# Filling TensorE's waits in the first stage of a two-layer decoder trunk with zero products, and taking that stage in another order

## The reference, cut to what matters

```
mod_all = jnp.einsum('bd,lde->lbe', jax.nn.silu(c), w_mod) + b_mod[:, None]
shift1, scale1, gate1, shift2, scale2, gate2 = jnp.split(mod_all[i], N_MOD, axis=-1)
h = rms_norm(x, norm_g[i, 0]) * (1.0 + scale1[:, None]) + shift1[:, None]
# pooling mixer: causal means over 2, 4, 8, 16 tokens minus the token, by group of 256 channels
pooled = jnp.stack([mean_w(h_g) - h_g ...], axis=2)
y = jnp.einsum('bsgc,gce->bsge', pooled, w_grp).reshape(B, S, D) * scale
x = x + gate1[:, None] * rms_norm(y, norm_g[i, 1])
h = rms_norm(x, norm_g[i, 2]) * (1.0 + scale2[:, None]) + shift2[:, None]
y = swiglu(h, ffn_w_gu[j], ffn_w_down[j])
```

## Time and profile before

| | |
|---|---|
| median of 3 runs | 1278.63 us (1278.04 to 1280.4) |
| profiled execution | 1280.07 us |
| its span, first to last instruction | 1278.2 us |
| mean granted TensorE clock | 0.991 |
| PE busy | 1249.0 us (98%) |
| DVE, ACT, POOL busy | 387.3, 214.7, 109.8 us |
| moved by DMA | 477.47 MB, mean 374 GB/s |
| first product of the SwiGLU starts | 70.39 us |

### The profile page before, as it was taken

How to read it: one execution, slowest core, us unless ns; L and a number is a source line. 1 busy time by engine, 2 the same in 40 slices (tenths; PEclk the granted TensorE clock), 3 DMA queues, 4 the chain that set the end, 5 groups by cost and what they waited for, 6 DMA issues and landing times.

```text
span 1278.2 us, 31266 instructions
## 1 busy us (share of the span) xinstructions
PE 1249.0 (98%) x14625; PEld 779.1 (61%) x14625; DVE 387.3 (30%) x591; ACT 214.7 (17%) x320; POOL 109.8 (9%) x134
## 2 busy tenths in 40 slices
PE   6799999999999999999999999999999999999997
PEld 3589999989774354545455454554545545454555
DVE  1567778979872110101101011010101201011012
ACT  3253333474842000000000000000000000000001
POOL 4220000010030000020010010002001000200100
PEclk9899999999999999999999999999999999999999
DMA  9998998959379999999999999999999999999980
GB/s 371 414 358 295 334 333 305 364 197 395 123 245 420 425 423 425 424 402 424 424 407 424 424 409 411 424 409 404 423 421 396 422 424 412 404 424 415 399 355 36
DMA packets 114055, 477.47 MB, mean 374 GB/s; under 512 B 10944, under 2 KB 37280, under 8 KB 113792
## 3 DMA queue, kind: packets, MB, share of 16 engines
q1 hardware_dynamic: 106112, 457.29, 89.1%
q0 software_dynamic: 7664, 17.87, 4.6%
q10 hardware_dynamic: 144, 0.26, 0.1%
HBM read 465.79 MB, written 11.16 MB: 373 GB/s over the span
## 4 chain that ended last, share of the span: by engine, by line
PE 95%; DVE 2%; ACT 1%; POOL 1%; DMA 1%; issue 1%; SPq 0%; DVEq 0%; ACTq 0%
PE ps L2421 23%; PE ps L2407 23%; PE ps L2396 23%; PE ps L1927 7%; PE ps L1928 7%; PE ps L1929 7%; PE ps L1952 1%; PE ps L2014 1%; PE ps L1911 1%; DMA raw<-w_mod 1%; DVE wlo L1572 1%; PE ps L2205 1%; PE ps L1975 0%; PE ps L2035 0%; PE ps L2350 0%
## 5 line engine op out<-in xcount | busy, mean ns | idle before, releaser
L1799 DVE TENSOR_TENSOR act_in<-act_in,ps 128x1344 f32<-128x1344 f32 x16 | 24.9, 1555 | 527.1 <-PE ps L2407 527.1
L1927 PE MATMUL ps<-thi,whi 128*128 128x256 f32 x480 | 136.0, 283 | 0.8 <-DVE wlo L1421 0.8
L1928 PE MATMUL ps<-tlo,whi 128*128 128x256 f32 x480 | 135.8, 283 | 0.0
L1929 PE MATMUL ps<-thi,wlo 128*128 128x256 f32 x480 | 135.8, 283 | 0.0
L2396 PE MATMUL ps<-raw,turned_in 128*32 128x448 f32 x1296 | 123.7, 539 | 0.0
L2407 PE MATMUL ps<-ring_w,turned_in 128*32 128x448 f32 x1248 | 120.6, 539 | 0.0
L2421 PE MATMUL ps<-ring_w,turned_act 128*32 128x256 f32 x2016 | 117.2, 379 | 0.0
L2421 PE MATMUL ps<-raw,turned_act 128*32 128x256 f32 x2016 | 115.5, 379 | 0.0
L1220 ACT ACTIVATE act_in<-ps 128x1344 f32<-128x1344 f32 x16 | 20.7, 1292 | 548.6 <-PE ps L2396 548.6
L1290 DVE TENSOR_TENSOR wlo<-raw,whi 128x2048 fp32r<-128x2048 f32 x41 | 92.9, 2289 | 32.7 <-ACT whi L901 32.7
L2421 PEld LDWEIGHTS ps<-raw,turned_act 128*32 128x32 f32 x2016 | 82.4, 110 | 33.5 <-issue 3.5
(11 more groups left out here) (324 smaller groups left out, 1332.0 us busy)
## 6 DMA issues: line engine op xcount, KB each, us to landing
raw<-moe_w_gu SPq DMA_DIRECT2D x96, 896.0 KB, 12.9
ring_w<-moe_w_gu SPq DMA_DIRECT2D x96, 896.0 KB, 13.0
raw<-w_mod SPq DMA_DIRECT2D x84, 512.0 KB, 5.7
rows<-moe_w_gu SPq DMA_DIRECT2D x48, 896.0 KB
raw<-moe_w_down SPq DMA_DIRECT2D x48, 896.0 KB, 13.9
ring_w<-moe_w_down SPq DMA_DIRECT2D x48, 896.0 KB, 13.4
raw<-ffn_w_gu SPq DMA_DIRECT2D x44, 512.0 KB, 5.6
rows<-moe_w_down SPq DMA_DIRECT2D x24, 896.0 KB
```

What stands on the lines that cost most here:

```text
L1799: dve.tensor_tensor(act_3, act_3, gate_up_ps(1), ALU.mult).then_inc(e_act, 1)
L1927: pe.matmul(out, a_hi, b_hi, start=start, stop=False, skip_group_check=check)
L1928: pe.matmul(out, a_hi, b_lo, start=False, stop=False, skip_group_check=check)
L1929: return pe.matmul(out, a_lo, b_hi, start=False, stop=stop, skip_group_check=check)
```

## The change

All of it is in the first stage.

- The tokens `xs` are loaded ahead of unit 0, the band matrices right after unit 0, and a unit waits until the unit two before it has landed, not three.
- `zeros` is cleared by DVE, at its begin, and no longer by POOL. PE begins with 56 zero products, and 19 further calls of `keep_clock`, of 6 to 40 products, stand between the pieces of its work, all into bank 3. Some stand behind a wait of their own.
- On PE the pooling goes ahead of units 2 and 3, of the second `spread` and of the columns of scale1; the units 4, 5, 7, 9 and 12 to 15 are taken one at a time between waits; unit 9 now comes behind a wait for `gate_done` 2; `turn_columns(4)` goes ahead of `turn(0)`.
- On ACT the squares go first, and the copies of the two spread vectors go behind the normalized tokens and ahead of scale1's sum.
- The sums of the vectors and the row of gate1 lie in other banks of the product memory.

```diff
-HEAD_BANK = {1: 7, 0: 0, 4: 2, 3: 3}
+HEAD_BANK = {1: 1, 0: 0, 4: 0, 3: 1}
-ROW_BANK = [[None, None, 0, None, None, 2], [None, None, 0, 2, 6, 6]]
+ROW_BANK = [[None, None, 2, None, None, 2], [None, None, 0, 2, 6, 6]]
...
-                if 3 <= r < RAW + WIDE:
-                    _, landed, n = head_slot(r - 3)
+                if 2 <= r < RAW + WIDE:
+                    _, landed, n = head_slot(r - 2)
                     sp.wait_ge(landed, n)
...
+            sp.dma_start(xs[:, :, :], x[0].rearrange("(t p) d -> p t d", p=P)).then_inc(x_loaded, 16)
             for r, (g, pair) in enumerate(HEAD):
                 load(r, 0, mod_unit(0, g, pair))
-                if r == 1:
+                if r == 0:
                     sp.dma_start(pool_band, pool_in.rearrange("p (g s) -> p g s", g=4)).then_inc(pool_loaded[0], 16)
-                    sp.dma_start(xs[:, :, :], x[0].rearrange("(t p) d -> p t d", p=P)).then_inc(x_loaded, 16)
...
+            for t in range(T):
+                square_x(0, t)
             act.wait_ge(cols_ps, 1)
...
-            for t in range(T):
-                square_x(0, t)
-            copy_wide(0, 2, rows[:, 6, :])
             for t in range(T):
                 normalize_tile(0, t)
+            copy_wide(0, 2, rows[:, 6, :])
+            copy_wide(1, 2, gain[:, 1, :])
             head_sum(1)
...
-            copy_wide(1, 1, gain[:, 1, :])
             square_mixed(1)
...
+            dve.memset(zeros[:, :], 0.0).then_inc(zeros_ready, 1)
             dve.wait_ge(pool_loaded[0], 16)
...
+            pe.wait_ge(zeros_ready, 1)
+            keep_clock(4, 56)
+            pe.wait_ge(silu_ready, 1)
+            head_units((0,))
...
+            spread(0, 2)
+            head_units((1,))
+            keep_clock(4, 12)
+            pe.wait_ge(pool_placed, 2)
+            pe.wait_ge(h_ready, T)
...
+            for b in range(4):
+                pooled(b)
+            head_units((2,))
+            pe.wait_ge(wide_ready, 1)
+            pe.wait_ge(first_gain_loaded, 16)
+            spread(1, 2)
+            head_units((3,))
+            turn_columns(1)
...
             mix(MIX_ORDER[0])
-            head_units((7, 9))
+            head_units((5,))
+            keep_clock(3, 12)
+            head_units((7,))
+            keep_clock(3, 40)
+            pe.wait_ge(gate_done, 2)
+            keep_clock(3, 8)
+            head_units((9,))
+            keep_clock(3, 6)
             turn_columns(0)
+            keep_clock(3, 12)
             pe.wait_ge(pooled_done, KC)
             mix(MIX_ORDER[1])
-            pe.wait_ge(wide_ready, 2)
+            pe.wait_ge(gate_done, 3)
+            keep_clock(3, 16)
             pe.wait_ge(gate_done, 4)
             row_sum(0, 2)
...
             pe.wait_ge(gated, T)
+            keep_clock(3, 12)
+            head_units((15,))
+            turn_columns(4)
+            keep_clock(3, 12)
             turn(0)
-            turn_columns(4)
-            head_units(range(16, 17))
+            head_units((16,))
+            keep_clock(3, 12)
             turn(1)
-            head_units(range(17, 20))
+            head_units((17,))
+            keep_clock(3, 16)
+            head_units((18,))
+            keep_clock(3, 16)
+            head_units((19,))
+            keep_clock(3, 6)
             turn_columns(3)
```

More of the change, by code:

```diff
@@ L730, in _ @@
             pool.memset(rows[:, 5, :], 0.0).then_inc(rows_zeroed, 1)
-            pool.memset(zeros[:, :], 0.0).then_inc(zeros_ready, 1)
             pool.wait_ge(rows_zeroed, 2)
@@ L935, in _ @@
             act.activation(silu_c[:, :], silu_c[:, :], ACT.Silu).then_inc(silu_ready, 1)
[L937 to L940, removed]
             def copy_wide(i, b, dst):
@@ L949, in _ @@
                 square_x(0, t)
-            copy_wide(0, 2, rows[:, 6, :])
+            act.wait_ge(cols_ps, 1)
+            act.copy(cols[:, :, :], ps[:, 6, 0:9 * KC].rearrange("p (i k) -> p i k", k=KC)).then_inc(cols_ready, 1)
+            act.wait_ge(dist_ps, 1)
+            act.activation(bias_row[:, 0:S], ps[0:NH, 5, 0:S], ACT.Copy, scale=HD ** 0.5).then_inc(dist_ready, 1)
             for t in range(T):
                 normalize_tile(0, t)
+            copy_wide(0, 2, rows[:, 6, :])
+            copy_wide(1, 2, gain[:, 1, :])
             head_sum(1)
@@ L1963, in turn_columns @@
                 mm.then_inc(col_ps, 1)
[L1965 to L1971, removed]
             def spread(i, b):
@@ L1976, in spread, with pooled @@
                 mm.then_inc(wide_ps, 1)
[L1978 to L1993, removed]
+            def pooled(b):
                 for t in range(T):
@@ L2004, in _ @@
                 mm.then_inc(pooled_ps, 1)
-            pe.wait_ge(first_gain_loaded, 16)
-            spread(1, 1)
-            head_units((4, 5))
             def mix(t):
@@ L2017, in mix @@
                 mm.then_inc(mix_ps, 1)
+            pe.wait_ge(zeros_ready, 1)
+            keep_clock(4, 56)
+            pe.wait_ge(silu_ready, 1)
+            head_units((0,))
+            pe.wait_ge(consts_loaded, 16)
+            pe.wait_ge(mcol_loaded, 64)
+            pe.transpose(ps[:, 6, 0:9 * KC], mcol, ident[0:9 * KC, 0:9 * KC]).then_inc(cols_ps, 1)
+            pe.wait_ge(small_loaded, 32)
+            pe.matmul(ps[0:NH, 5, 0:S], relb, onehot, start=True, stop=True).then_inc(dist_ps, 1)
+            pe.wait_ge(scale_loaded, 16)
+            spread(0, 2)
[3 more added lines that the diff above has]
+            pe.wait_ge(h_ready, T)
+            pe.wait_ge(cols_ready, 1)
+            pe.wait_ge(dist_ready, 2)
+            for b in range(4):
[6 more added lines that the diff above has]
+            turn_columns(1)
+            pe.wait_ge(wide_ready, 2)
+            keep_clock(3, 8)
+            pe.wait_ge(col_ready, 1)
+            for g in range(4):
+                mm = pe.matmul(ps[:, 1, g * EDGE:g * EDGE + EDGE], ones, pool_band[:, g, 0:EDGE], start=(g == 0), stop=True,
+                               skip_group_check=True)
+            mm.then_inc(m1_ps, 1)
+            keep_clock(3, 16)
+            head_units((4,))
+            pe.wait_ge(pooled_ready, KC // 2)
+            keep_clock(3, 12)
+            pe.wait_ge(pooled_ready, KC)
             pe.wait_ge(scale_folded, 2)
-            pe.wait_ge(pooled_ready, KC)
             mix(MIX_ORDER[0])
-            head_units((7, 9))
+            head_units((5,))
[3 more added lines that the diff above has]
+            pe.wait_ge(gate_done, 2)
+            keep_clock(3, 8)
+            head_units((9,))
+            keep_clock(3, 6)
             turn_columns(0)
+            keep_clock(3, 12)
             pe.wait_ge(pooled_done, KC)
             mix(MIX_ORDER[1])
-            pe.wait_ge(wide_ready, 2)
+            pe.wait_ge(gate_done, 3)
+            keep_clock(3, 16)
             pe.wait_ge(gate_done, 4)
@@ L2037, in turn @@
                         mm.then_inc(ht_ps, 1)
-            head_units(range(12, 16))
+            pe.wait_ge(col_ready, 2)
+            head_units((12,))
+            pe.wait_ge(row_done, done_rank(0, 2))
+            keep_clock(3, 10)
+            head_units((13,))
+            pe.wait_ge(gated, 1)
+            keep_clock(3, 16)
+            head_units((14,))
+            pe.wait_ge(x_done, 1)
+            keep_clock(3, 12)
             pe.wait_ge(gated, T)
+            keep_clock(3, 12)
+            head_units((15,))
+            turn_columns(4)
+            keep_clock(3, 12)
             turn(0)
-            turn_columns(4)
-            head_units(range(16, 17))
+            head_units((16,))
+            keep_clock(3, 12)
             turn(1)
-            head_units(range(17, 20))
+            head_units((17,))
+            keep_clock(3, 16)
+            head_units((18,))
+            keep_clock(3, 16)
+            head_units((19,))
+            keep_clock(3, 6)
             turn_columns(3)
-            pe.wait_ge(zeros_ready, 1)
-            keep_clock(0, 24)
+            keep_clock(3, 24)
             def ffn_gate_up(s, r, q, first=False):
```

2 lines of the change are left out of this document (1 added, 1 removed).

## The result

| | before | after |
|---|---|---|
| median of 5 executions | 1279.83 us (1278.04 to 1280.90) | 1291.68 us (1287.03 to 1292.77) |
| ratio of the times (over all executions) | 1 | 1.0088, 95% interval 1.0074 to 1.0102 |
| profiled execution, span | 1280.07 us, 1278.2 us | 1292.77 us, 1290.9 us |
| mean granted clock | 0.991 | 0.987 |
| first product of the SwiGLU | 70.39 us | 83.06 us |

The sign was forecast, the size was not: +11.9 us in the medians, outside the range that ended at 1287.0. The spans differ by 12.7 us and the SwiGLU's first products by 12.67 us, so the whole loss arises in the first stage and nothing behind it gives any back.

The account below looks back on a forecast made before the run. PE was taken to bound the end of the chain, with a mixed DVE and PE chain pacing the first stage. 2.9 + 0.7 + 0.8 = +4.4 us turned the median 1278.63 into 1283.0 us, range 1279.3 to 1287.0.

Parts of the forecast that it names:

- the term of 2.9: Start up to the first mix: mix at 31.3 us in the middle case of the clock, a shift of +2.9 us.
- so the eight copies lie open: Ahead of the first mix: ACT's eight scaled copies, no longer hidden under the pooling, take 3.6 us after scale1's columns.
- The first mix to unit 9: PE from the first mix's start to unit 9's end, 60 zeros included: 10.1 us in the changed order.
- The high clock gives back some 3.5 us here: End of the stage, from turn_columns(4): the high clock's gain of 3.5 us is spent by 56 zeros and the wait.
- +0.8 for the pause: PE idle ahead of turn_columns(4): the clock may fall, costing 0 to 1.7 us; half taken, up to 2 if transposes don't count.
- the +0.7: End of the stage at the high clock: 9.35 us from 58.46 gives 67.8 against 67.09, +0.7 us.
- I cost this at 0: Loads with two units in flight: 0 us, with ends of -2 and +3 us.
- The middle at 0: Second mix, zeros by the gate work, units 12 to 15 under the residual, later-freed SwiGLU weights: each 0 us.
- The clock did not stay up: Rival: clock stays high through the start, 1279.5 to 1280.3 us, no change; chance 0.28.
- The loads made nothing faster: Rival: two in flight land unit 8 earlier, at 31.2, giving 1276.0 us; chance 0.07.
- that rival: Rival: zeros do not raise the clock, so they cost more and the time is near 1295 us; chance 0.04.
- starve nothing that the time depends on: Rival: two units in flight starve the load queues, +3 us on the forecast, 1286.0 us; chance 0.04.

Follow-up runs that it names:

- the turn ahead again: Changed kernel with turn_columns(4) (scale2's columns) moved back behind turn(0), the first transposes: 1285.82 us, 1.0050 of the kernel before.
- The order without zeros: Changed kernel with every keep_clock call removed except the last one of 24, all waits kept: 1281.98 us, 1.0026 of the kernel before.
- filling the pause: Changed kernel with 44 more zero products between unit 15 and turn_columns(4): 1288.17 us, 1.0057 of the kernel before.
- the kernel with early zeros: Kernel before plus 60 zeros in PE's last long wait and 52, 28, 24 and 18 around units 0 to 3: 1279.70 us, ratio 0.9992.
- the kernel whose end has no zeros: Changed kernel without the zeros (12, 12, 16, 16, 6) behind turn_columns(4), the last 24 kept: 1288.07 us, 1.0064 of the kernel before.
- the one with the loads alone: Kernel before with only the change's loads: tokens first, band matrices after unit 0, two units in flight: 1281.50 us, ratio 1.0023.

## Why the prediction was right in sign and short in size

**The start, +5.5 us beyond the term of 2.9.** This is the term that was mis-sized: the mix was forecast for 31.3 and came at 36.84. The step that failed in it is "so the eight copies lie open", which started the mix 3.6 us after scale1's columns, with a clock that stays high from the pooling on. The clock fell again ahead of those columns, and behind them PE has work of its own that the step did not count at all: eight zeros, the edge sums, 16 zeros, unit 4 and 12 zeros. From the start of the copies to the mix it was 5.96 us, 2.4 more than forecast, all of it PE. The 36 zeros behind the columns took 3.3 us (30.22 to 31.03, 32.70 to 34.50, 36.16 to 36.84) and were costed at nothing without naming their cover (the prediction counts 72 zeros up to the second mix where 126 stand). At the high clock the five pieces would be 0.5 + 0.9 + 0.9 + 0.94 + 0.7 = 3.9 us, nearly under the 3.6 of the copies, and the profile of the turn ahead again shows just that: from the copies' start (29.16) to the mix (32.76) it was 3.60 us. So the uncounted work cost what it did because the clock was down. The rest of the 5.5: unit 0 ended at 11.70, not 10.3, on the low clock (1.4 us); the pooling took 5.09 for 4.1 (1.0); and from unit 3 to scale1's columns it was 2.1 for 1.4 (0.7), with the clock falling ahead of 29.35. The sum is that of the profiled execution, one of the seven among eleven with a mean clock of 0.987 or 0.988; with the clock up from 20 us on the start was off by 1.5 us only (32.76 for 31.3). The order without zeros starts its mix 3.7 us earlier though its clock fell as well, so what costs is the two together, zeros on the list and a fall ahead of them. Why the clock falls there in some executions and not in others stays open, and the zeros ahead of the mix were not taken out by themselves.

**The first mix to unit 9: right.** Forecast 10.1 us, measured 10.2 (36.84 to 47.01). Taking the 60 zeros out gave 0.26 to 0.34% back.

**"The high clock gives back some 3.5 us here", with +0.8 for the pause.** The mechanism was right and the size wrong. (By its own pieces the high clock gives back 3.9 us, not 3.5; the +0.7 is right as added up.) PE stood 2.58 us ahead of `turn_columns(4)`, released by ACT's copy, as forecast. From there the forecast had 9.35 us at the high clock to the end of unit 19, and it took 12.8 (66.91 to 79.71), so the clock cost 3.45 us and not 0.8; filling the pause measured 3.0, and profiles with a shorter fall 1.6. I had taken a half of a bound that was itself a size too small: 1.7 us is what 3.4 us of low clock cost, and 6.8 us were low. The upper end of 2 that the prediction named was nearer and still short.

**The sum.** 2.9 and 5.5, then 0.7 and 0.8 and 2.65: 12.55, of 12.7 measured.

**"I cost this at 0", the loads.** Two in flight: right (1.0001). The tokens in front: unit 0's landing near 9.4 was right (9.84), and it was in the term of 2.9 for the new order, but at 0 as an edit of its own it was wrong. Alone it cost 0.15%: in the kernel before, too, PE's own list from unit 0 to unit 9 had little slack for a late start (unit 0 came 2.9 us later and the mix 2.25).

**The middle at 0: right.** From the turned columns to scale2's copy the distance to before stays at 8.5 us, though 78 zeros lie in it: 12 behind the columns, 16 behind DVE's third part, 50 between the units. The reason given for the SwiGLU's weights, "the queue holds more than that", was wrong: between 71 and 74 us the queues moved 106, 0 and 13 GB/s. The 0 held all the same, since in the 50 us behind it no engine waited for a transfer, and that was luck.

**The rivals.** The clock did not stay up; unit 0 already ran slow in this profile, and the first spread took 3.78 us in every profile of the changed kernel's beginning. The loads made nothing faster: DVE's wait for unit 8 ended at 36.79, for 34.51. The queues moved only 156 GB/s between 35 and 36 us. With three units in flight the changed kernel had that landing at 34.36, so the 2.3 us go with the smaller distance (one profile each); they cost nothing, since DVE then stood 8.82 us for PE. Zeros do raise the clock (last section), so that rival fell too. Two in flight do delay landings, and starve nothing that the time depends on.

## What to carry to other kernels

A filler product is free only where its engine waits for something else, and this has to be shown row by row: here 60 of them in one real pause gained 0.15%, and 176 of the changed kernel's lay between pieces of a list that hardly paused. With the low clock that they met, the zeros made some 0.6% of its 0.9%; the other 0.2 to 0.3% came with the loads, the tokens ahead of the first weights above all. Cost them at their own length at the low clock if they follow a fall, and cost every instruction between the last input and the waited-for product, not only the engine that feeds it. And when an instruction with a late input is moved ahead of others, price the pause by what the clock does behind it as well, 1.6 to 3.0 us here behind a pause of 2.6. And before one profile is read as the price of an edit, look at another of the same list: here six of them differ by 4 us at one and the same instruction.

## What the runs showed of the hardware that was not expected

- A busy PE is not a PE at the full clock. From 10 to 20 us it was busy all the time at 0.50, with units of 32 stationary columns, a spread of one row, and 12 zeros; in the kernel with early zeros the 24 zeros behind a one-row spread took 2.56 us and the unit behind them 1.94.
- Zero products alone raise the clock: of the 56 in front of unit 0, 12 began between 4 and 5 us and 20 between 5 and 6. What a pause does to it is not fixed: behind one of 3.57 us unit 0 took 1.93 in the changed kernel, and behind one of 3.95 us it took 1.07 in the kernel whose end has no zeros (PE's timeline):

```profile
9.61 1.07 PE L1949 MATMUL ps<-raw,silu_c 128*32 128x256 f32 x16 [3.95 <-DMA raw<-w_mod]
```

- The record of the clock shows 1.00 over the first 20 us of the kernel before and of the one with the loads alone, where every unit takes 1.93 us in both. Only the durations tell there.
- The same kernel lies 5 us apart from one execution to the next by where its clock falls. The Trainium skill ("TensorE: Matmul & The Clock Gate", Part 1: The HAM clock gate) says that the length of a slow start varies from run to run of one kernel; the traces here agree: the 56 zeros that begin the changed kernel took from 4.60 to 6.05 us over seven profiles, and its times lie between 1287.0 and 1292.8 us.
